# Rows of a projection turned by VectorE in 32x32 blocks and carried by DMAs within SBUF, in place of TensorE transposes

## What is computed

```python
def even_layer(x, mem, ...):               # layer 0
    c_q, c_kv, k_pe, qkv_b, q_mem, gate = split_cols(rms_norm(x, norm_g) @ w_in, EVEN_SPLITS)
    o_a = causal_attention_qblocks(q_a, k_a, v_a, 192 ** -0.5)      # "mla", 8 heads, from c_q and c_kv
    o_b = moba_attention(apply_rope(q_b), apply_rope(k_b), v_b)     # "moba", 8 heads of 128
    o_m = memory_attention(q_mem, mem, mem_norm_g, w_mem_kv)        # "mem", 4 heads, 256 memory rows
    return x + (concat(o_a, o_b, o_m) * silu(gate)) @ w_out

def odd_layer(x, mem, ...):                # layer 1
    o_c = banded_attention(apply_rope(q_c), k_c, v_c)               # "swa", 16 heads of 64
    o_d = dilated_attention(apply_rope(q_d), apply_rope(k_d), v_d)  # "dil", 6 heads of 128
    o_m = memory_attention(q_mem, mem, mem_norm_g, w_mem_kv)        # "mem"
    return x + (concat(o_c, o_d, o_m) * silu(gate)) @ w_out

def hybrid_layer(x, ...):                  # layers 2 and 3
    (qa, ka, va, za, qi, ki, wi, ub, zb, qc, kc, vc, zc, gates) = split(rms_norm_2(x, norm_w) @ w_in)
    y_a = (dsa_attention(qa, ka, va, qi, ki, wi, 64) * silu(za)) @ w_a_out   # "dsa"; 16 index heads choose 64 keys
    y_b = (conformer_conv(ub, ...) * silu(zb)) @ w_b_out                     # 31 taps, 1024 channels
    y_c = (stick_breaking_attention(qc, kc, vc) * silu(zc)) @ w_c_out        # "stick", 8 heads
    return x + (g0 * y_a + g1 * y_b + g2 * y_c) @ w_out                      # g = sigmoid(gates)
```

## Time and profile before

| | |
|---|---|
| median of 3 executions | 3167.98 us (3167.77 to 3168.29) |
| the profiled execution | 3168.17 us |
| its span | 3166.4 us |
| TensorE matmuls busy | 3144.5 us, 15096 of them |
| VectorE busy | 1985.2 us |
| ScalarE busy | 1599.3 us |
| DMA queue of SyncE and loads | 297888 packets, 557.65 MB, 59.1% of 16 engines |

### The profile page before, as it was taken

One profiled execution on the slowest core, in us unless ns is written; L12 is line 12 of the kernel. 1 busy time (PEld: TensorE's weight loads), 2 busy tenths in 40 slices (PEclk: granted clock), 3 DMA queues, 4 the chain that ended last, 5 costly groups with the idle time before them and its releaser, 6 DMA issues. The chain is left out here.

```text
span 3166.4 us, 38304 instructions
## 1 busy us (share of the span) xinstructions
PE 3144.5 (99%) x15096; PEld 2640.6 (83%) x15096; DVE 1985.2 (63%) x3006; ACT 1599.3 (51%) x2253; POOL 7.1 (0%) x18
## 2 busy tenths in 40 slices
PE   8999999999999999999999999999999999999998
PEld 7888888888988888888888888888888888888886
DVE  5555455665455799975555555558998655555555
ACT  7655454565455544555544444444455655444443
POOL 0000000000000000000000000000000000000000
PEclk9999999999999999999999999999999999999999
DMA  9556565645566655555566666565555566666664
GB/s 307 164 155 173 168 197 168 205 140 161 153 200 188 180 178 166 174 153 171 169 188 194 189 194 193 181 191 176 166 170 166 149 180 180 193 201 192 195 185 151
DMA packets 301955, 570.34 MB, mean 180 GB/s; under 512 B 18096, under 2 KB 36672, under 8 KB 301392
## 3 DMA queue, kind: packets, MB, share of 16 engines
q1 hardware_dynamic: 297888, 557.65, 59.1%
q10 hardware_dynamic: 3040, 6.42, 0.6%
q0 software_dynamic: 848, 3.83, 0.4%
HBM read 565.73 MB, written 2.10 MB: 179 GB/s over the span
## 5 line engine op out<-in xcount | busy, mean ns | idle before, releaser
L134 DVE TENSOR_TENSOR wl<-raw,wh 128x1024 fp32r<-128x1024 f32 (+3 forms) x1088 | 1287.6, 1188 | 923.0 <-ACT wh L123 920.7
L123 ACT ACTIVATE wh<-raw 128x1024 fp32r<-128x1024 f32 (+3 forms) x1088 | 1119.3, 1032 | 1323.0 <-PE gp L108 1307.8
L108 PE MATMUL gp<-wh,Hh 128*128 128x512 f32 (+3 forms) x2400 | 925.0, 385 | 0.1
L108 PE MATMUL gp<-wh,Hl 128*128 128x512 f32 (+3 forms) x2400 | 911.8, 380 | 0.0
L108 PE MATMUL gp<-wl,Hh 128*128 128x512 f32 (+3 forms) x2400 | 911.1, 380 | 0.0
L108 PE MATMUL gp<-wh,Yh 128*128 128x512 f32 (+2 forms) x1952 | 762.4, 391 | 8.8 <-DVE wl L134 8.8
L108 PE MATMUL gp<-wh,Yl 128*128 128x512 f32 (+2 forms) x1952 | 755.2, 387 | 0.0
L108 PE MATMUL gp<-wl,Yh 128*128 128x512 f32 (+2 forms) x1952 | 755.0, 387 | 0.0
L108 PEld LDWEIGHTS gp<-wh,Hl 128*128 128x128 f32 x2400 | 451.3, 188 | 86.0
L108 PEld LDWEIGHTS gp<-wh,Hh 128*128 128x128 f32 x2400 | 451.6, 188 | 82.8 <-issue 1.3
L108 PEld LDWEIGHTS gp<-wl,Hh 128*128 128x128 f32 x2400 | 451.9, 188 | 81.4
(11 more groups left out here) (124 smaller groups left out, 1213.5 us busy)
## 6 DMA issues: line engine op xcount, KB each, us to landing
raw<-in_w_in SPq DMA_DIRECT2D x560, 512.0 KB, 3.8
raw<-in_ev_w_in SPq DMA_DIRECT2D x104, 512.0 KB, 3.8
raw<-in_od_w_in SPq DMA_DIRECT2D x80, 512.0 KB, 3.7
raw<-in_w_out SPq DMA_DIRECT2D x64, 512.0 KB, 3.9
raw<-in_ev_w_out SPq DMA_DIRECT2D x40, 512.0 KB, 3.7
raw<-in_od_w_out SPq DMA_DIRECT2D x36, 512.0 KB, 3.7
raw<-in_w_b_out SPq DMA_DIRECT2D x32, 512.0 KB, 4.7
raw<-in_w_a_out SPq DMA_DIRECT2D x32, 512.0 KB, 4.8
```

The costliest lines, as they stand in the source:

```text
L108: return self.e.matmul(out, l, r, start=start, stop=stop)
L123: return self.e.activation(out, in_, func, **kw)
L134: return self.sketch(157 + size(a) * 1.042) if self.e is None else self.e.tensor_tensor(out, a, b, op)
```

## The change

For kinds nat and mk the TensorE transposes and the copies out of PSUM are gone. VectorE transposes the nat buffer in place, 32x32 block by block (`flip`). Then SyncE issues, for every pair of 32-partition groups (a, b) and half t, one DMA within SBUF that carries the blocks to their places in the target (`move`): 32 partitions, up to four runs of 32 numbers each. That is 32 DMAs per projection, 16 KB each where there are four column blocks. A move waits for its flip, for the target to be free, for the move before it in order, and for the move four before it to have landed. The nat buffer is given back when the last of the DMAs has landed. The planner puts 60 ns of queue time for each of these DMAs as well.

```diff
+    def flip(self, out, in_):
+        return self.sketch(157 + size(in_) * 1.042) if self.e is None else self.e.transpose(out, in_)
+
     def dma_start(self, dst, src):
         if self.e is None:
-            self.plan.step.dma = size(dst) * dst.shape[0] * 4
+            self.plan.step.dma = (self.plan.step.dma or 0) + size(dst) * dst.shape[0] * 4
             return self.sketch(60)
...
         def turned(gm, dst, c0, blocks):
+            gm.target = dst[:, 0:256 * blocks]
...
             turned(gm, self.mkT, 0, 4)
-            gm.copier = "dve"
...
+        self.moves = [gm for gm in self.gemms if gm.kind in ("nat", "mk")]
+        for m, gm in enumerate(self.moves):
+            gm.moved = m
...
+    def moved_at(self, m):
+        return self.s_move[m % 4].at((m, 3, 3, 1))
+
     def turned_at(self, gm):
+        if gm.moved is not None:
+            return self.moved_at(gm.moved)
...
+    def move(m):
+        gm = P.moves[m]
+        g, s, src = gm.g, P.s_move[m % 4], P.nat.buf(gm.g)
+        if m:
+            e.behind("move", m - 1)
+        e.wait_ge(*P.v_flip.at(g))
+        for w in P.clear_turn(gm, 0):
+            e.wait_ge(*w)
+        if m >= 4:
+            e.wait_ge(*P.moved_at(m - 4))
+        blocks = gm.n // 128
+        for a in range(4):
+            for b in range(4):
+                x = src[32 * a:32 * a + 32, :, 0:gm.n].rearrange("p t (h b r) -> p t h b r", b=4, r=32)
+                y = gm.target[32 * b:32 * b + 32, :].rearrange("p (h t a r) -> p t h a r", h=blocks, t=2, a=4)
+                for t in range(2):
+                    e.dma_start(y[:, t, :, a, :], x[:, t, :, b, :]).then_inc(*s.up((m, a, b, t), 16))
+        P.nat.give(g, s, (m, 3, 3, 1))
...
+    def flip(g):
+        gm = P.gemms[g]
+        b = P.nat.buf(g)[:, :, 0:gm.n]
+        if gm.rope:
+            e.wait_ge(*P.v_rope.at((g, 1 if gm.rope[5] == 1 else 0, 3)))
+        e.wait_ge(*P.a_evac.at((g, "end")))
+        e.flip(b, b).then_inc(*P.v_flip.up(g))
...
-        for u in range(len(gm.turns)):
+        if gm.moved is not None:
+            add("dve", "flip", g)
+            add("sp", "move", gm.moved)
+        for u in range(0 if gm.moved is not None else len(gm.turns)):
             add("pe", "turn", g, u)
             add("dve" if gm.copier == "dve" else "act", "turned", g, u)
```

More of the change, by code:

```diff
@@ L296, in __init__ @@
         self.kind, self.gid, self.part = kind, gid, part
-        self.turns, self.rope, self.copier = [], None, "act"
+        self.turns, self.rope, self.copier, self.moved = [], None, "act", None
 class Group:
@@ L387, in signals @@
         self.s_cc = sig("s_cc")
+        self.s_move = [sig(f"s_move{i}") for i in range(4)]
         self.s_out = [sig(f"s_out{i}") for i in range(4)]
@@ L399, in signals @@
         self.v_rope, self.v_turned, self.v_gate = sig("v_rope"), sig("v_turned"), sig("v_gate")
+        self.v_flip = sig("v_flip")
         self.v_max, self.v_rl, self.v_y, self.v_wi = sig("v_max"), sig("v_rl"), sig("v_y"), sig("v_wi")
@@ L831, in stored @@
         e.wait_ge(*P.s_out[n].at("o"))
-    return {"load_memt": load_memt, "load_mem2": load_mem2, "raw": raw, "store": store, "stored": stored}
+    return {"load_memt": load_memt, "load_mem2": load_mem2, "raw": raw, "move": move, "store": store, "stored": stored}
 def pool_program(P, e):
@@ L1799, in dve_program @@
     return {"gains": gains, "weigh": weigh, "square_last": square_last, "lo": lo, "in_lo": in_lo, "stat": stat, "refine": refine, "rope": rope,
-            "turned": turned, "gate": gate, "smax": smax, "recip": recip, "head_out": head_out, "log_beta": log_beta,
+            "turned": turned, "flip": flip, "gate": gate, "smax": smax, "recip": recip, "head_out": head_out, "log_beta": log_beta,
             "log_keep": log_keep, "log_after": log_after, "a_strict": a_strict, "stick_out": stick_out,
```

## The result

The changed kernel takes 3730.01 us (3725.27 to 3731.15), the kernel before 3168.14 beside it: ratio 1.1771, 95% interval 1.175 to 1.1791. It is 562 us slower, where 301 were forecast. The time lies inside the stated range of 3300 to 3750, near its top, and above the likeliest case's own range, which ended at 3621.

What follows compares the result with a forecast made beforehand. TensorE was taken to bound the kernel, busy 3144.5 of 3166.4 us. -29 (transposes) + 259 (reader stands) + 38 (clock) + 33 (late loads) = +301 us on 3168 gave 3469 us, range 3300 to 3750.

Steps and rivals of the forecast that it cites:

- likeliest case: Whole kernel: SyncE's issues set the moves' pace; +301 us, 3469 us, own range 3353 to 3621, chance 0.63.
- p: Time SyncE's queue spends per small DMA of a move, gap included: taken as 0.44 us.
- What is removed: TensorE's stream: 264 transposes gone at 0.111 us each, 29.3 us saved; evictions and copies on other engines worth nothing.
- VectorE: 34 in-place block transposes added at 1.22 us each, 42 us covered by idle time; twice 1.22 as upper bound.
- SyncE's queue: 32 issues per move share the queue with weight loads: 0.44 us per DMA, 14.1 us per move.
- The reader's stand: TensorE waits at first matmuls reading moved rows: 10.8 us at each of 24 moves, 259 us.
- Weight loads: Loads queued behind ten moves not read at once: TensorE waits 2.6 us at nine, 9.4 at group 8's narrow q; 33 us.
- the slack: Time a weight load can be late before TensorE waits: 10.4 us, at group 8's narrow q 4.3.
- The clock: TensorE's slow matmuls after each reader's stand: 24 x 1.6 = 38 us, bounds 0 and 54.
- Rival 1: DMA engines set the moves' pace, 0.83 us per DMA: +709, 3877 us; chance 0.19 with what lies between.
- Rival 2: SyncE passes small DMAs in far less than 0.37 us, moves hide: only the gain left, 3139 us; chance 0.06.
- Rival 3: Readers stand later in TensorE's order, each stand shrinks to the load lateness: +66, 3234 us; chance 0.09.

Runs made afterwards that it cites:

- e1: Changed kernel with the flip writing straight into the target and the 32 DMAs per projection left out (heads read wrong rows): 3138.43 us, ratio 0.9906 to before.
- e8: Changed kernel with moves issued by GpSimd instead of SyncE and the planner told 600 ns per DMA: 3140.94 us, ratio 0.9913 to the kernel before.
- e10: Changed kernel with only the second half of the rows (t = 1) moved for kind nat, 16 DMAs instead of 32; kind mk keeps 32: 3392.12 us.

## Why the prediction was right, and where it was off

The mechanism held, down to which 24 moves made a reader stand and which 10 made a load late; the total was 261 us short. The time lies in the stated range because that left room for dearer issues (up to p about 0.70); the likeliest case's own range, with p up to 0.52, missed it by 109 us, and the sign named for it, issues 0.42 to 0.45 apart, did not show. The errors did not cancel: nearly all lie on the slow side. The measured terms add up on the kernel without moves: 3138.4 + 387.5 (readers) + 117 (loads) + 88.5 (TensorE busy 3203.6 against 3115.1) = 3731.4, for 3730.0.

- **What is removed**: 29.3 us forecast, 30.1 measured (e1).
- **VectorE**: a flip takes 1.240 us, against 1.22 taken. The Trainium skill, page "VectorE: DVE Perf Modes", section "The three transpose paths", led to an estimate of 2.5 us; the measurement decides, and it is half of that.
- **SyncE's queue**: the term that was mis-sized. I took p = 0.44 us because issues took 0.368 us "whatever it loads". All those rows had their source in HBM. (The issues at the start that the earlier trace rows leaves out go up to 0.67 us; I had read 0.40 to 0.47.) Measured: 0.60 + 0.04, a move of 20.6 us instead of 14.1. With 0.644 the forecast's own formulas give 24 x 17.2 + 38 + 9 x 9.1 + 16 - 29 = +520, 3688 us; this one number is 219 of the missing 261 us.
- **The reader's stand**: 10.8 us forecast, 16.1 measured. The longer issues add 6.3; the rest, -1.0, is the landing (1.8 for 2.3), against a split in front of the flip that took 1.1 in the example instead of 0.3, and the readers' places.
- **Weight loads**: at the nine 2.6 us forecast, 11.2 measured. 6.5 of this is again p. SyncE also waited 1.3 us per flip (43.6 us in 34 waits) instead of 0.3, and what is left would put the slack nearer 9.4 than 10.4 us. At the narrow q it was 9.4 us forecast, 16.2 measured; with p = 0.644 the forecast's formula gives 15.9.
- **The clock**: 38 us forecast, with an upper bound of 54; 88 measured. I priced the step behind a stand in wide matmuls and only for the readers. The slow steps behind the load wait at 264.22 cost 1.8 us (268.06 - 264.22 = 3.84 us for nine steps that take 2.04 at 0.227), near the 1.6 I had. Behind a reader's stand come 16 small matmuls, 4.9 us instead of 2.4, and the slow start of the next fill. The ten load waits pay too. The granted clock shows it: 0.925 over the span, 0.999 before; 0.50 in the window above. The Trainium skill, "TensorE: Matmul & The Clock Gate", Part 1, calls 1.2 GHz the level after idleness; the trace agrees.
- **Rival 1** gave 3877 us, 147 off where the likeliest case was 261 off, but that is luck: the engines are 16% busy during a move, 2.5 engine-us per us for 199 runs, 0.013 us a run, where the rival had taken 0.104 and the likeliest case 0.036.
- **Rival 2** fell with the issue of 0.60. The section "Issuing engines are not separate DMA queues" of the Trainium skill's "DMA: Bandwidth & Descriptors" calls issue time usually small against the DMA, so that another issuing engine saves little; here another queue saved 218 us alone and 415 with the order mended, because the 32 issues held SyncE's queue for 20.6 us with the DMA engines 16% busy. **Rival 3** fell: all 24 readers stood.

## What to carry to other kernels

Many small DMAs are paid for in the queue that issues them: count them, take the price from an issue of the same kind (source place above all), and ask what stands behind them in that queue. When a step gets slower, tell the planner, or its readers are written too early and a strict queue stands for them. Mending one of two such causes shows only a part of what they cost (164 or 218 of 579 us here); queue and order had to be mended together to turn +18% into -0.9%.

## What the runs showed of the hardware that was not expected

- A DMA issued by SyncE out of SBUF takes 0.60 us of the queue, out of HBM 0.43 with the same pattern; GpSimd's issue of the SBUF one takes 0.549, less than SyncE's (its 32 issues in 17.3 us against 20.6). The data land later after GpSimd's issue: a median of 3.1 us in e8 against 1.8 in the changed kernel.
- A stand of 6 us costs TensorE nearly as much in slow matmuls afterwards (70.6 us over the 31 stands of e10, 2.3 each) as one of 16 (88.5 over 34, 2.6 each).
- VectorE's block transpose of 128x1024 fp32 in place takes 1.240 us, about what a subtraction of that size takes (1.22).
